# A decoder layer on one core: the output projection's first three weight units interleaved, closing squares summed by matmuls, gate rows by transposes

## What is computed

```python
h = rmsnorm(x, norm1_g)
proj = h @ w_in                       # columns for three head groups
o_dn  = gated_deltanet(...)           # 6 heads, chunked delta rule
o_dil = dilated_attention(...)        # 4 heads
o_nsa = nsa_attention(...)            # 6 heads, 2 shared K/V groups
x = x + concat(o_dn, o_dil, o_nsa) @ w_out
h = rmsnorm(x, norm2_g)
u_gate, u_val = split(causal_dwconv(h @ ffn_up, ffn_conv))
x = x + (silu(u_gate) * u_val) @ ffn_down
return rmsnorm(x, final_g)
```

## Time and profile before

| | us |
|---|---|
| median of 3 runs | 2627.38 (2626.01 to 2631.46) |
| the profiled execution's own time | 2631.8 |
| its span, first to last instruction | 2630.0 |
| TensorE busy | 2545.9 (97%) |
| VectorE, ScalarE busy | 1362.5, 875.7 |
| mean granted TensorE clock | 0.984 of full speed |

### The profile page before, as it was taken

The page is one execution under the profiler, slowest core; times in us unless marked ns, Lnnn a source line. Parts: engine busy times, 40 slices in busy tenths (PEclk is TensorE's granted clock), DMA queues, the critical chain, the costliest instruction groups (busy, mean ns, idle before and its releaser), DMA issues.

```text
span 2630.0 us, 33127 instructions
## 1 busy us (share of the span) xinstructions
PE 2545.9 (97%) x11784; PEld 2077.6 (79%) x11784; DVE 1362.5 (52%) x2313; ACT 875.7 (33%) x1614; POOL 0.3 (0%) x6
## 2 busy tenths in 40 slices
PE   8999999899999988999999999999999999999996
PEld 5888888677887656888888888888888888888884
DVE  6667666434345673355444444444444444444446
ACT  5444444223233452243232323232323232323232
POOL 0000000000000000000000000000000000000000
PEclk9999999899999988999999999999999999999998
DMA  4411111212333123223222222222222222222222
GB/s 163 151 62 68 51 65 58 82 74 82 121 128 139 40 96 149 100 95 108 97 96 96 96 96 96 96 96 96 96 96 96 96 96 96 96 96 96 96 96 80
DMA packets 41594, 251.73 MB, mean 96 GB/s; under 512 B 5392, under 2 KB 5648, under 8 KB 13884
## 3 DMA queue, kind: packets, MB, share of 16 engines
q1 hardware_dynamic: 41532, 250.90, 26.5%
HBM read 242.97 MB, written 13.15 MB: 97 GB/s over the span
## 4 chain that ended last, share of the span: by engine, by line
PE 54%; DVE 1%; ACT 0%; issue 0%; DVEq 0%; ACTq 0%
PE bank L231 36%; PE bank L1672 18%; DVE x_t L1821 0%; DVE head_out L1752 0%; ACT head_out L1795 0%; DVE rms_row L1818 0%; PE bank L1774 0%; DVE x_t L1744 0%; PE bank L1659 0%; ACT rms_row L1797 0%; DVEq L1634 0%; ACTq L1794 0%; DVEq L1801 0%
## 5 line engine op out<-in xcount | busy, mean ns | idle before, releaser
L231 PE MATMUL bank<-h_hi,w_hi 128*128 128x512 f32 x2176 | 886.5, 407 | 22.0 <-DVE w_lo L191 15.6
L231 PE MATMUL bank<-h_lo,w_hi 128*128 128x512 f32 x2176 | 854.3, 393 | 0.0
L231 PE MATMUL bank<-h_hi,w_lo 128*128 128x512 f32 x2176 | 853.8, 392 | 0.0
L231 PEld LDWEIGHTS bank<-h_hi,w_hi 128*128 128x128 f32 x2176 | 413.2, 190 | 113.0 <-issue 12.5
L231 PEld LDWEIGHTS bank<-h_lo,w_hi 128*128 128x128 f32 x2176 | 412.1, 189 | 88.8
L231 PEld LDWEIGHTS bank<-h_hi,w_lo 128*128 128x128 f32 x2176 | 413.0, 190 | 85.7 <-issue 5.3
L182 ACT ACTIVATE w_hi<-w_raw_far 128x512 fp32r<-128x512 f32 x528 | 307.2, 624 | 439.5 <-PE bank L1672 274.7
L191 DVE TENSOR_TENSOR w_lo<-w_raw_far,w_hi 128x512 fp32r<-128x512 f32 x528 | 331.0, 684 | 124.0 <-ACT w_hi L182 122.7
L191 DVE TENSOR_TENSOR w_lo<-w_raw,w_hi 128x512 fp32r<-128x512 f32 x312 | 200.7, 685 | 144.2 <-ACT w_hi L182 144.1
L1672 PE MATMUL bank<-h_hi,w_hi 128*128 128x512 f32 x704 | 274.4, 390 | 1.0 <-DVE x_t L1744 1.0
L1672 PE MATMUL bank<-h_lo,w_hi 128*128 128x512 f32 x704 | 273.9, 389 | 0.0
(11 more groups left out here) (284 smaller groups left out, 1887.7 us busy)
## 6 DMA issues: line engine op xcount, KB each, us to landing
w_raw_far<-in_weights SPq DMA_DIRECT2D x132, 1024.0 KB, 4.8
w_raw<-in_weights SPq DMA_DIRECT2D x77, 1024.0 KB, 4.8
x_t<-in_x_t SPq DMA_DIRECT2D x7, 1024.0 KB, 10.2
bias_rows<-bias_row SPq DMA_DIRECT2D x10, 512.0 KB, 7.2
out<-x_t SPq DMA_DIRECT2D x8, 512.0 KB, 2.7
mix_scratch<-head_out SPq DMA_DIRECT2D x14, 256.0 KB
nsa_tab<-bias_rows SPq DMA_DIRECT2D x6, 448.0 KB, 7.6
h_lo<-mix_scratch SPq DMA_DIRECT2D x1, 2560.0 KB, 12.2
```

The source lines that it names most:

```text
L231: m = nc.tensor.matmul(PB[pb][:], a[:, s, k], b, start=(kt == 0 and n == 0), stop=(kt == KT - 1 and n == 2))
```

## The change

It has three parts.

- **The front.** `WO_QUARTERS` packs units 0, 1 and 2 of the output weights by quarters: the first six as before, then unit 2's quarters 0 to 2, then quarter 3 of all three. `WO_EARLY` keeps its 24 steps. The last NSA round splits 8 quarters instead of 4 (`left`), so unit 2 is split in it, and SP issues one more `load_unit` there. Behind the barrier the loop over whole units starts at 3. The split of a unit stands at d = 0 and d = 2 to 14 instead of d = 1 to 15, the residuals of units 0 to 2 wait for other counts, and the waits for x and for the gains stand further back.
- **The end.** Squares of the last group go to 8 places in `w_raw`; VectorE sums 12 of them, and the last 4 are added by matmuls with ones, in one accumulation with the sum. The last store of two tiles becomes two stores of one.
- **Gate rows.** `gate_step` copies the column that is already cumulated, and `dn_pe` transposes it.

```diff
@@ -59,2 +59,4 @@
 
+WO_QUARTERS = ((0, 0), (1, 0), (0, 1), (1, 1), (0, 2), (1, 2), (2, 0), (2, 1), (2, 2), (0, 3), (1, 3), (2, 3))
+
 LEVELS = (2, 4, 8, 16, 32, 64)
@@ -526,4 +528,3 @@
                 for b in range(TB):
-                    m = nc.tensor.matmul(W[0][:, b * P:(b + 1) * P], B["gb"][:, b * P:(b + 1) * P],
-                                         cst[:, K_TRI, :], start=True, stop=True)
+                    m = nc.tensor.transpose(W[0][:, b * P:(b + 1) * P], B["gb"][:, b * P:(b + 1) * P], ident)
                 m.then_inc(grow_ps, 1)
@@ -649,3 +650,3 @@
 
-                link(dve, nc.vector.tensor_copy(hg[:], of_head(tok, h)[:, C_G, :]))
+                link(dve, nc.vector.tensor_copy(hg[:], of_head(tok, h)[:, C_GC, :]))
                 nc.vector.tensor_copy(v3(B["gb"][:]), bc(hg[:], P)).then_inc(g_rep, 1)
@@ -1094,3 +1095,3 @@
 
-        WO_PAIR = [(u, kt) for q in range(4) for u in range(2) for kt in range(4 * q, 4 * q + 4)]
+        WO_FRONT = [(u, kt) for u, q in WO_QUARTERS for kt in range(4 * q, 4 * q + 4)]
 
@@ -1156,3 +1157,3 @@
             WO_FILLS = (0,) * 5 + (1,) + (2,) * 10
-            WO_EARLY = WO_PAIR[:3 * len(WO_PAIR) // 4]
+            WO_EARLY = WO_FRONT[:24]
             MIX_AT = 2
@@ -1235,3 +1236,3 @@
             def nsa_act(act, r, last):
-                left = [4 if last else 8]
+                left = [8]
 
@@ -1386,2 +1387,3 @@
                         load_unit(sp)
+                        load_unit(sp)
                     for g in range(NSA_G if r < NSA_R - 1 else 0):
@@ -1573,3 +1575,3 @@
         def residual(dve, d):
-            dve.wait_ge(q_used, Q5 + (4 * (d + 1) if d else 7))
+            dve.wait_ge(q_used, Q5 + (4 * (d + 1) if d > 1 else 10 + d))
             nc.vector.tensor_tensor(x1[:, d, :], x1[:, d, :], PB[d % 4][:], ALU.add).then_inc(wo_free, 1)
@@ -1590,6 +1592,6 @@
             def _(pe):
-                for u, kt in WO_PAIR[len(WO_EARLY):]:
+                for u, kt in WO_FRONT[len(WO_EARLY):]:
                     pe.wait_ge(m_lo, len(MIX_EARLY) if kt < MIX_LATE[0] else KT)
                     project(pe, u, kt)
-                for d in range(2, KT):
+                for d in range(3, KT):
                     pe.wait_ge(wo_free, d + 1)
@@ -1602,5 +1604,4 @@
                     mix_hi(act, i)
-                act.wait_ge(g2_in, 32)
                 for d in range(KT):
-                    split_hi(act, 4 if d else 0)
+                    split_hi(act, 4 if d not in (1, KT - 1) else 0)
                     if d < KT - 1:
@@ -1608,2 +1609,3 @@
                         square(act, d)
+                act.wait_ge(g2_in, 32)
                 act.wait_ge(lo_done, 4 * FFN_UNIT)
@@ -1619,6 +1621,6 @@
                 nc.vector.memset(ssq[:], 0.0).then_inc(ss_v, 1)
-                dve.wait_ge(xr_in, 64)
-                dve.wait_ge(g2_in, 32)
                 for d in range(KT):
-                    split_lo(dve, 4 if d else 0)
+                    split_lo(dve, 4 if d not in (1, KT - 1) else 0)
+                    if d == 0:
+                        dve.wait_ge(xr_in, 64)
                     if d < KT - 1:
@@ -1626,2 +1628,3 @@
                         add_square(dve, d)
+                dve.wait_ge(g2_in, 32)
                 for d in range(H2A):
@@ -1643,2 +1646,9 @@
                                           "r2_root r2_ok").split())
+            SQ_SUMMED, SQ_SLOTS = KT - 4, 8
+            OUT_PIECES = (*((d, d + 2) for d in range(0, KT - 2, 2)), (KT - 2, KT - 1), (KT - 1, KT))
+
+            def fin_square(d):
+                k = d % SQ_SLOTS
+                return w_raw[:, k // 4, k % 4 * SEQ:(k % 4 + 1) * SEQ]
+
             (fin_sq, fin_ss, fin_ps, fin_root, fin_ok, fin_v, out_s) = (
@@ -1744,3 +1754,3 @@
                         nc.vector.tensor_tensor(dst, dst, W[b][:], ALU.add).then_inc(dn_free, 1)
-                        if last and (c or b):
+                        if last and 0 < 4 * c + b <= SQ_SUMMED:
                             square_sum(dve, 4 * c + b - 1)
@@ -1751,5 +1761,5 @@
                     dve.wait_ge(fin_ss, d)
-                    nc.vector.tensor_tensor(ssq[:], ssq[:], sq[:], ALU.add).then_inc(fin_ss, 1)
+                    nc.vector.tensor_tensor(ssq[:], ssq[:], fin_square(d), ALU.add).then_inc(fin_ss, 1)
                 else:
-                    nc.vector.tensor_copy(ssq[:], sq[:]).then_inc(fin_ss, 1)
+                    nc.vector.tensor_copy(ssq[:], fin_square(d)).then_inc(fin_ss, 1)
 
@@ -1759,6 +1769,6 @@
                 load_units(sp, (Q7 + GQ * N_GROUP) // 4)
-                for d in range(0, KT, 2):
-                    sp.wait_ge(fin_v, d + 2)
-                    sp.dma_start(t["out"][:, d:d + 2, :], x1[:, d:d + 2, :]).then_inc(out_s, 16)
-                sp.wait_ge(out_s, 16 * (KT // 2))
+                for a, e in OUT_PIECES:
+                    sp.wait_ge(fin_v, e)
+                    sp.dma_start(t["out"][:, a:e, :], x1[:, a:e, :]).then_inc(out_s, 16)
+                sp.wait_ge(out_s, 16 * len(OUT_PIECES))
 
@@ -1771,5 +1781,8 @@
                 down_pe(pe, N_GROUP - 1)
-                pe.wait_ge(fin_ss, KT)
-                pe.wait_ge(dn_free, 4 + 16 * N_GROUP)
-                nc.tensor.matmul(W[0][:], ones, ssq[:], start=True, stop=True).then_inc(fin_ps, 1)
+                pe.wait_ge(fin_ss, SQ_SUMMED)
+                nc.tensor.matmul(PB[0][:], ones, ssq[:], start=True, stop=False)
+                for d in range(SQ_SUMMED, KT):
+                    pe.wait_ge(fin_sq, d + 1)
+                    m = nc.tensor.matmul(PB[0][:], ones, fin_square(d), start=False, stop=(d == KT - 1))
+                m.then_inc(fin_ps, 1)
 
@@ -1792,7 +1805,7 @@
                     act.wait_ge(dn_free, 4 + 16 * (N_GROUP - 1) + d + 1)
-                    if d:
-                        act.wait_ge(fin_ss, d)
-                    nc.scalar.activation(sq[:], x1[:, d, :], ACT.Square).then_inc(fin_sq, 1)
+                    if d >= SQ_SLOTS:
+                        act.wait_ge(fin_ss, d - SQ_SLOTS + 1)
+                    nc.scalar.activation(fin_square(d), x1[:, d, :], ACT.Square).then_inc(fin_sq, 1)
                 act.wait_ge(fin_ps, 1)
-                nc.scalar.activation(r2[:], W[0][:], ACT.Sqrt, bias=eps_t[:], scale=1.0 / D_MODEL).then_inc(fin_root, 1)
+                nc.scalar.activation(r2[:], PB[0][:], ACT.Sqrt, bias=eps_t[:], scale=1.0 / D_MODEL).then_inc(fin_root, 1)
 
@@ -1815,3 +1828,2 @@
                 down_dve(dve, N_GROUP - 1, Q7 + GQ * N_GROUP - DNQ, True)
-                square_sum(dve, KT - 1)
                 dve.wait_ge(fin_root, 1)
@@ -1901,5 +1913,5 @@
         columns(w_out, d * P)
-    pair = [u.reshape(P, 4, QW) for u in units[-KT:-KT + 2]]
-    for i in range(2):
-        units[i - KT] = np.stack([pair[u][:, 2 * i + q] for q in range(2) for u in range(2)], axis=1).reshape(P, -1)
+    front = [u.reshape(P, 4, QW) for u in units[-KT:-KT + 3]]
+    for i in range(3):
+        units[i - KT] = np.stack([front[u][:, q] for u, q in WO_QUARTERS[4 * i:4 * i + 4]], axis=1).reshape(P, -1)
 
```

## The result

Six runs of the changed kernel, in turn with six of the kernel before on the same chip: 2607.09 us in the median (2606.37 to 2608.76) against 2629.23 us (2626.01 to 2631.46). The ratio is 0.9917, with a 95% interval of 0.9907 to 0.9928: 22.1 us less, between 18.9 and 24.5. The profiled execution of the changed kernel took 2608.76 us, with a span of 2606.8; the one of before took 2631.8 and 2630.0.

What follows compares the result with a forecast made beforehand. TensorE's stream and its standstills were taken to bound the kernel (busy 2545.9 of 2630.0 us). Terms 13.1 + 2.8 + 1.1 + 2.9 + 0.4 = 20.3 us off the 2627.38 median gave 2607.1, range 2602 to 2614.

Steps and rivals of the forecast that it cites:

- Front, 13.1 us: Start of the output projection: unit 2's tiles first behind the barrier bring unit 3's residual 13.1 us sooner.
- the second slow stretch: Output projection, behind TensorE's 5.19 us wait: 48 matmuls at clock 0.79 take 13.94 us over 10.88, costed at 2.8 us.
- the second wait: Output projection: TensorE's 5.19 us wait, until 1009.31, for unit 2's split queued behind the first residual; claimed to go.
- The cost at nothing: Attention stage's end and output projection: four added splits, SP's extra load and later residuals were claimed to delay nothing.
- rival 1: At the barrier the clock falls in the remaining gap all the same, costing 3.1 us: gain 17.2, time 2610.2; chance 0.14.
- Gate rows, 2.8 us: DeltaNet: 4 matmuls become 4 transposes in each of 6 heads, saving 0.46 us a head, 2.8 us in all.
- Rival 2: DeltaNet gives its share back because VectorE's recurrence sets when a head ends: gain 17.5, time 2609.9; chance 0.08.
- rival 5: DeltaNet: added transposes drop each head's opening to half clock, six heads lose 39 us, time 2646, slower; chance 0.02.
- Pieces, 1.1 us: Last down projection: eight square buffers let VectorE's fourth add come 0.48 us sooner per piece, 1.1 us in all.
- Root, 2.9 us: Closing norm: 12 squares summed by VectorE and five full-clock closing matmuls start the root 2.9 us sooner.
- rival 3: Closing norm: the five closing matmuls run at half clock, root 3.0 us later: gain 14.4, time 2613.0; chance 0.03.
- Store, 0.4 us: Program's end: halving the last output store gives between 0 and 0.66 us, taken as 0.4.

## Why the prediction was right, and where not

The time came out where it was put, 2607.1, and each part's place was right. Point by point:

- **Front, 13.1 us:** 13.0 in the two traces, 13.1 by undoing it. The start came 1.84 sooner (forecast 1.96). The numbers given for the second slow stretch, 13.94 over 10.88 us, make 3.06 and not 2.8: 49 records, and 0.17 us until the result is there, are in it. The sum doesn't hang on that, since it is taken from unit 3's end. The step that was wrong is the split of the rest: "5.19 for the second wait, 3.1 and 2.8 for what the two slow stretches cost". With the clock held behind the first gap, the second wait grew by 3.6 us, to 8.79, and the total stayed. The cost at nothing of the four splits, of SP's load and of the later residuals held for TensorE; so did the clock behind 1.4 us of standstill at the barrier in the changed kernel's two traces (rival 1 did not occur).
- **Gate rows, 2.8 us:** 0.47 us a head against 0.46, 2.8 in all. Rival 2 did not occur, nor did rival 5. The upper bound of 0.53 us a head has no row behind it. What the sum left out is that the heads' length moves what follows: undoing this part cost 6.3 us and not 2.8, 1.1 to 1.3 of it at the start of the dilated heads.
- **Pieces, 1.1 us:** the four pieces' first banks are 10.91, 11.47 and 11.50 us apart in the changed trace, against 11.05, 12.00 and 11.97: 1.14 us.
- **Root, 2.9 us:** 9.25 - 6.33 = 2.92 us. The closing matmuls ran at full clock (rival 3 did not occur). The mechanism is split between the buffers (1.4 for the turns, and 0.95 for the lone matmul's clock in the one trace with buffers alone) and the closing matmuls (0.6), which the sum did not say.
- **Store, 0.4 us:** 0. The step that failed is the price of halving, 0.4 out of "256 KB / 398 GB/s = 0.66", taken from the bytes of the last store as if that store moved alone. The reason given, that the stores are as much bound by bandwidth as by the last scaling, is neither shown nor refuted. In all three ways of cutting, 3.1 us follow the last scaling, with 0.86 MB still moving. Whether the scalings' 392 GB/s or DMA's 398 set that, the runs don't show.
- **The base.** The sum of what is shown is 13.1 + 2.8 + 1.1 + 2.9 = 19.9 us, and the two medians lie 22.1 us apart. The prediction subtracted from 2627.38, the median of three runs; the six runs of the comparison have 2629.23. So the hit is two deviations that cancel: the base was 1.9 us higher than assumed, and the gain 2.2 us larger than the parts. In the two profiles the excess is 3.3 us, all of it ahead of the last value matmul; the half-clock sums of 48 and 41 us would cover it, but 0.8 us of it is the dilated heads' start (14.0 against 13.3 us), so the two overlap and the shares are open. The kernels with longer heads show such an excess too, of 1.1 to 3.5 us. That the change's own 2.8 us brought the excess is likely from them, but only the direction is shown. The mechanisms were right; the hit within 0.1 us is luck.

## What to carry to other kernels

Where one engine sets the time, read each gap on it together with the clock behind it and the next wait: a slow stretch ahead of a wait costs nothing by itself, and only undoing the whole part gives its worth. Order the work behind a barrier so that what needs nothing new stands first, and give two engines that take turns over one buffer a few buffers before moving work to a third. Take profiles twice before a difference of a few us in untouched code gets a cause, look for a wait that has grown before it is put down to the clock, and measure a part by marks around it, which repeated here to 0.1 us while the whole varied by 6.6 us between runs of one kernel.

## What the runs showed of the hardware that was not expected

- After a gap of 3.25 us TensorE's granted clock fell in one trace (0.65 over the next 24 matmuls) and held at 1.00 in two others, with nearly the same instructions around it. Repetitions of one kernel, too, differ in where the clock falls.
- Work of 2.5 us added in DeltaNet cost 4.5 us, of 5.3 us 6.4, and of 2.8 by matmuls 6.3: the time of this kernel is not the sum of its instructions' costs to better than 2 to 3 us. With such work added the first weights behind DeltaNet kept ScalarE waiting for 7.2 to 9.0 us instead of 6.0 to 6.5.
- A store of 256 KB landed after 2.0 us with nothing under way and after 2.7 behind stores of 512 KB, and the program ended 3.1 us behind the last scaling in each of the three ways of cutting the output.
